# Lists of 112 places with the tokens in steps of seven, in the expert loop of a decoder trunk

## The chip, the cores and the metric

The kernel runs on one core of a Trainium2 chip. The metric is the device time of one execution in microseconds (us); the median of several executions is compared. The engines are TensorE (PE, with its weight loads as PEld), VectorE (DVE), ScalarE (ACT), GpSimd (POOL) and SyncE (SP, which issues DMAs). The core has 16 DMA engines.

## What is computed

Two layers, each a token mixer (three kinds of attention), a norm, a mixture of experts and a second norm, for 512 tokens of width 1024 in float32. The part that matters here is the mixture of experts:

```
scores = sigmoid(x @ router_w)                    # 512 x 64
idx    = top_k(scores + router_bias, 8)           # 8 of 64 experts for each token
gates  = scores[idx] / sum * 2.5
for each expert e, for the tokens routed to it:
    y = (silu(h @ w1[e]) * (h @ w3[e])) @ w2[e]   # 1024 -> 256 -> 1024
    y = y * gate
out = sum over a token's 8 experts + shared expert
```

In all 512 x 8 = 4096 pairs of a token and an expert arise in each layer, 64 for an expert on average. The weights of one expert are three matrices of 1024 x 256 float32, 1.049 MB each.

## The kernel before

The program runs `_setup` once, and then for each of the two layers `_projections`, `_attention`, `_mix_and_route`, `_experts` and `_second_norm`. Each is a block in which every engine has its own instruction stream, ordered against the others by semaphores.

**Lists.** Each expert has a list of `CAP` = 100 places (line 54). `_mix_and_route` writes into `posm` the rank of each token within each expert's tokens (0, 1, 2, ..., or a negative number if it isn't routed there). For an expert, DVE compares this rank with the constants in `number` (line 1400: `hot` is 1 where the rank equals the place's number); `number` comes from `np.arange(CAP)` in `_constants` (line 106), so the token of rank r stands at place r. A matmul of `hot` with the table `parts` (line 1320, and one with `ones` at 1323) then gives for every place the token's row in `x1_rows`, its destination row in `y_rows` and its gate; a place without a token gets an index that is out of bounds. DVE writes the indices (lines 1408 and 1410). If an expert had more than `CAP` tokens, the expert loop would run again for the rest (`passes`, from the largest count, line 1133); here one pass is run per layer.

**The loop.** `_experts` runs 64 steps, with `Turn(x)` for the expert of the step. The parts of one step lie on different engines:

- SP, `load` (lines 1257 to 1266): the three weight matrices of expert x into slot x mod 4, `w1` and `w3` (1261, 1262) when `up_made` says that PE is through with the slot's last `w1` and `w3`, `w2` (1266) when `down_made` says so. SP's stream is in order, so the `w1` of x + 1 stands behind the wait of `w2` of x.
- POOL, `gather` (line 1287): an indirect DMA of the rows in the list, 4 KB each, from `x1_rows` in HBM, three steps ahead; `put` (line 1295): an indirect DMA of the result rows to `y_rows` in HBM, two steps behind. Rows of places without a token are left out by the bounds check.
- ACT: `up_hi` in two halves (line 1481) rounds the weights to the type that PE multiplies fast (float32r), `hidden_hi` (1502), `gates` (1508, silu), `rows_hi` (1495, 1496), `dn_hi` (1488), `scaled` (1516, multiplies by the gate). In a step they stand in the order up_hi(x+1, 0), hidden_hi(x-1), gates(x), rows_hi(x+1), up_hi(x+1, 1), dn_hi(x), scaled(x-1).
- DVE: `hots` (1400), `indices`, `hidden_lo` (1448), `up_lo` (1429), `hide` (1422), `rows_lo` (1441), `dn_lo` (1434): the differences that the rounding leaves, and the product silu(up) * up.
- PE: `pick` (1320, 1323), `up` in two parts (1347 to 1349, 24 matmuls with 512 columns, three for each exact product: hi*hi, hi*lo, lo*hi), `turn_hidden` (1358, two transposes), `turn_rows` (1332, eight transposes), `down` (1372 to 1374, 12 matmuls). The list is on the stationary side of the matmuls and the weights move.

`silu` is a tile of its own of 128 x 2 x 256 (line 1236), `hidden` the same memory. `w_chunk` (line 1650) holds the first chunk of the projection weights: it is loaded in `_setup` and, for the next layer, in `_second_norm` (line 1570), and is read in `_projections`.

Of the kernel before, what the change touches and what calls it, by code (L numbers as in the profile page):

```python
# [33 lines left out]
P = 128  # L34
# [11 lines left out]
NE, TOPK, FF, SFF = 64, 8, 256, 256  # L46
# [4 lines left out]
MLA_SCALE = MQ ** -0.5  # L51
NEG = -1e30
TAKEN = -3e38
CAP = 100
MAX_PASSES = -(-SEQ // CAP)
NOT_ROUTED = 4096.0
ABSENT = 8192.0
# [27 lines left out]
def _buckets(distance):  # L85
    exact = N_BUCKETS // 2
    d = np.maximum(distance, 1).astype(np.float64)
    large = exact + (np.log(d / exact) / math.log(MAX_DISTANCE / exact) * (N_BUCKETS - exact)).astype(np.int64)
    return np.where(distance < exact, distance, np.minimum(large, N_BUCKETS - 1))


def _constants():
    k = np.arange(SPAN + 1)
    dist = SEQ - 1 - k
    causal = dist >= 0
    onehot = ((_buckets(np.maximum(dist, 0))[None, :] == np.arange(N_BUCKETS)[:, None]) & causal)
    count = sum(((dist % d == 0) & (dist <= w)).astype(np.int64) for w, d in DILATIONS)
    logcount = np.where(causal & (count > 0), np.log(np.maximum(count, 1)), NEG)
    addend = np.concatenate([np.repeat(logcount[None], H_DIL, 0),
                             np.repeat(np.where(causal, 0.0, NEG)[None], H_DSA, 0)])  # L100
    p = np.arange(P)
    inv = 10000.0 ** (-np.arange(0, ROPE, 2) / ROPE)
    square = np.concatenate([np.eye(P), p[:, None] < p[None, :], np.ones((P, P))], 1)
    absent = np.zeros((P, PART))
    absent[0, [IDX, DEST]] = ABSENT
    once = np.concatenate([np.eye(P)[::-1], np.repeat(np.arange(CAP)[None], P, 0), np.ones((P, CAP)), absent], 1)
    token = p[:, None] + P * np.arange(NT)[None]
    row = np.concatenate([np.repeat(inv[None], P, 0), token - ABSENT, TOPK * token - 1 - ABSENT], 1)
    mask = np.where(p[:, None] + (SEQ - P) - np.arange(SEQ)[None] >= 0, 0.0, NEG)
    f = np.float32  # L110
    return {
        "c_square": square.astype(f),
        "c_once": once.astype(f),
        "c_row": row.astype(f),
        "c_mask": mask.astype(f),
        "c_onehot": onehot.astype(f),
        "c_addend": (addend / SCALE).astype(f),
    }
# [31 lines left out]
def _setup(nc, d, sb):  # L150
    with ExitStack() as ctx:
# [10 lines left out]
        turns_i = ctx.enter_context(nc.sbuf_tensor("turns_i", [P, NT, ROPE // 2], I32))  # L162
        once = ctx.enter_context(nc.sbuf_tensor("once", [P, P + 2 * CAP + PART], F32))
        bias = ctx.enter_context(nc.sbuf_tensor("bias_set", [P, 10, SEQ], F32))
# [5 lines left out]
        with nc.Block() as block:  # L170
# [48 lines left out]
            def _(dve):  # L219
# [6 lines left out]
                dve.wait_ge(S["consts_in"], 32)  # L226
                dve.tensor_copy(sb["number"][:], once[:, P:P + CAP]).then_inc(S["numbers"], 1)
                dve.tensor_copy(sb["ones"][:], once[:, P + CAP:]).then_inc(S["numbers"], 1)
                dve.wait_ge(S["positions_in"], 32)
# [614 lines left out]
def _mix_and_route(nc, d, sb, l):  # L844
    with ExitStack() as ctx:
# [31 lines left out]
        with nc.Block() as block:  # L877
# [26 lines left out]
            def _(pool):  # L904
# [3 lines left out]
                for k in range(FIRST):  # L908
                    pool.wait_ge(S["index_ready"], k + 1)
                    pool.indirect_dma_start(sb["rows"][0:CAP, k, :], None, d["x1_rows"],  # L910
                                            bass.IndirectOffsetOnAxis(ap=index[0:CAP, k, 0:1], axis=0),
# [308 lines left out]
def _experts(nc, d, sb, l):  # L1220


    with ExitStack() as ctx:
# [4 lines left out]
        T = lambda name, shape, dt=F32: ctx.enter_context(nc.sbuf_tensor(name, shape, dt))  # L1228
# [4 lines left out]
        w2_hi = T("w2_hi", [P, 2, 2, D], F32R)  # L1233
        hot, index, gate = sb["hot"], sb["index"], sb["gate"]
        rows = sb["rows"]
        silu = T("silu", [P, 2, FF])
        hidden = silu
        rowsT_hi, rowsT_lo = T("rowsT_hi", [P, 2, KD, CAP], F32R), T("rowsT_lo", [P, 2, KD, CAP], F32R)
        hiddenT_hi, hiddenT_lo = T("hiddenT_hi", [P, 2, 2, CAP], F32R), T("hiddenT_lo", [P, 2, 2, CAP], F32R)
# [402 lines left out]
def trunk(nc, d, out):  # L1642
    with ExitStack() as ctx:
# [12 lines left out]
        with nc.Fori(0, DEPTH) as l:  # L1656
            with ExitStack() as kept:
                with ExitStack() as routed:
# [31 lines left out]
                    with nc.Fori(0, passes) as _:  # L1690
                        _experts(nc, d, sb, l)
# [24 lines left out]
```

## Time and profile before

| | |
|---|---|
| median of 3 runs | 2382.28 us (2380.42 to 2382.53) |
| the profiled execution's own time | 2378.7 us |
| its span, first to last instruction | 2376.9 us |
| PE busy | 2134.1 us (90%) |
| DVE busy | 1596.6 us (67%) |
| ACT busy | 1353.1 us (57%) |
| POOL busy | 610.4 us (26%) |
| moved by DMA | 595.90 MB, 251 GB/s over the span |
| row queue (q0, issued by POOL) | 46112 packets, 67.23 MB |

Busy shares are averages over stages with different limits. Matmuls are pipelined, so PE's busy time isn't PE at its peak. A wait says which event came last before an instruction started. In the slices of the page one digit stands for a fortieth of the span (59.4 us) and gives tenths of busy time.

### The profile page before, as it was taken

How to read it: one execution, taken by the hardware profiler on the slowest of the kernel's cores; microseconds unless marked ns; L12 is line 12 of the kernel's file. 1: busy time of each engine (PE TensorE's matmuls, PEld its weight loads, DVE VectorE, ACT ScalarE, POOL GpSimd, SP SyncE). 2: the span in 40 equal slices, each digit the busy share in tenths (PEclk: the TensorE clock that was granted, in tenths of full speed). 3: DMA queues.
4: the chain of work that ended last, by engine and by line, in shares of the span. 5: the costliest groups of instructions: out<-in, count | busy, mean ns of one | idle time of the engine just before them, and what ended most of it. 6: DMA issues, size and time to landing. Idle time of an engine off the chain costs nothing. (4 is left out here: it accounts for less than half of the span.)

```text
span 2376.9 us, 31682 instructions
## 1 busy us (share of the span) xinstructions
PE 2134.1 (90%) x10838; PEld 1571.8 (66%) x10838; DVE 1596.6 (67%) x2283; ACT 1353.1 (57%) x1754; POOL 610.4 (26%) x358
## 2 busy tenths in 40 slices
PE   6999999798999999897679999979999999999947
PEld 5788856576676666665367887457766676766633
DVE  2583434797888788786345924248988888888835
ACT  3533721587777777775034356126876777777731
POOL 0012000243333333333311020002433333333323
PEclk9999999899999999999789999999999999999989
DMA  6213043599999999998931230436999999999978
GB/s 197 77 45 151 2 167 125 194 354 346 347 348 337 345 333 336 341 334 297 380 106 54 63 133 3 173 148 249 356 346 345 339 344 338 341 339 339 345 279 333
DMA packets 148475, 595.90 MB, mean 251 GB/s; under 512 B 41957, under 2 KB 68069, under 8 KB 92313
## 3 DMA queue, kind: packets, MB, share of 16 engines
q1 hardware_dynamic: 102264, 527.41, 60.9%
q0 software_dynamic: 46112, 67.23, 9.1%
q8 instruction: 56, 0.92, 0.2%
q14 instruction: 43, 0.34, 0.0%
HBM read 571.23 MB, written 63.46 MB: 267 GB/s over the span
## 5 line engine op out<-in xcount | busy, mean ns | idle before, releaser
L1295 POOL DMA_INDIRECT y_rows<-y,index x128 | 297.0, 2320 | 798.5 <-ACT y L1516 790.0
L1347 PE MATMUL ps_up<-w_hi,rowsT_hi 128*100 128x512 f32 x1024 | 420.6, 411 | 37.3 <-issue 20.4
L1349 PE MATMUL ps_up<-w_hi,rowsT_lo 128*100 128x512 f32 x1024 | 405.8, 396 | 0.0
L1481 ACT CAST w_hi<-w_next 128x2048 fp32r<-128x2048 f32 x128 | 245.7, 1919 | 179.0 <-DMA w_next<-exp_w 169.5
L1481 ACT CAST w_hi<-w 128x2048 fp32r<-128x2048 f32 x128 | 245.3, 1918 | 132.8 <-DMA w<-exp_w 86.6
L1429 DVE TENSOR_TENSOR w_lo<-w,w_hi 128x2048 fp32r<-128x2048 f32 x128 | 292.3, 2285 | 35.9 <-ACT w_hi L1481 35.8
L1429 DVE TENSOR_TENSOR w_next_lo<-w_next,w_hi 128x2048 fp32r<-128x2048 f32 x128 | 292.1, 2282 | 6.3 <-ACT w_hi L1481 6.3
L1372 PE MATMUL ps_y<-w_hi,hiddenT_hi 128*100 128x512 f32 x512 | 211.3, 413 | 70.5 <-issue 66.2
L1347 PEld LDWEIGHTS ps_up<-w_hi,rowsT_hi 128*100 128x100 f32 x1024 | 173.7, 170 | 94.6 <-issue 41.8
L1287 POOL DMA_INDIRECT rows<-x_rows,index x128 | 189.0, 1476 | 122.5 <-issue 61.7
L1349 PEld LDWEIGHTS ps_up<-w_hi,rowsT_lo 128*100 128x100 f32 x1024 | 169.9, 166 | 68.9
L1348 PE MATMUL ps_up<-w_lo,rowsT_hi 128*100 128x512 f32 x512 | 204.5, 399 | 0.0
L1374 PE MATMUL ps_y<-w_hi,hiddenT_lo 128*100 128x512 f32 x512 | 204.1, 399 | 0.0
L1348 PE MATMUL ps_up<-w_next_lo,rowsT_hi 128*100 128x512 f32 x512 | 201.2, 393 | 0.0
L1448 DVE TENSOR_TENSOR hiddenT_lo<-ps_h,hiddenT_hi 128x200 fp32r<-128x200 f32 x128 | 46.9, 366 | 198.2 <-ACT hiddenT_hi L1502 197.7
L1372 PEld LDWEIGHTS ps_y<-w_hi,hiddenT_hi 128*100 128x100 f32 x512 | 86.9, 170 | 106.2 <-issue 75.5
L1332 PEld LDWEIGHTS ps_t<-ident,rows 100*128 100x128 f32 x1024 | 134.6, 202 | 29.9 <-issue 16.2
L1516 ACT ACTIVATE y<-ps_y,gate 100x1024 f32<-100x1024 f32 x128 | 145.2, 1134 | 12.1 <-DMA y_rows<-y,index 8.8
L1332 PE MATMUL ps_t<-ident,rows 100*128 100x100 f32 x1024 | 132.6, 273 | 16.1 <-PEq L139 16.1
L1434 DVE TENSOR_TENSOR w_next_lo<-w_next,w_hi 128x2048 fp32r<-128x2048 f32 x64 | 146.1, 2283 | 0.0
L1441 DVE TENSOR_TENSOR rowsT_lo<-ps_t,rowsT_hi 128x400 fp32r<-128x400 f32 x256 | 133.6, 563 | 0.0
L1488 ACT CAST w_hi<-w_next 128x2048 fp32r<-128x2048 f32 x64 | 123.2, 1925 | 0.0
(244 smaller groups left out, 4299.2 us busy)
## 6 DMA issues: line engine op xcount, KB each, us to landing
w_next<-exp_w SPq DMA_DIRECT2D x204, 1024.0 KB, 18.8
w<-exp_w SPq DMA_DIRECT2D x136, 1024.0 KB, 14.2
w_first<-exp_w SPq DMA_DIRECT2D x34, 1024.0 KB, 19.7
w_last<-exp_w SPq DMA_DIRECT2D x32, 1024.0 KB, 19.6
wbuf<-w_in SPq DMA_DIRECT2D x16, 1024.0 KB, 5.5
got<-y_rows SPq DMA_DIRECT2D x8, 2048.0 KB, 23.4
got<-y_rows SPq DMA_DIRECT2D x16, 1024.0 KB, 26.4
w_out_sb<-w_out SPq DMA_DIRECT2D x2, 4096.0 KB, 19.6
```

What stands on the lines that cost most here:

```text
L1287: pool.indirect_dma_start(rows[0:CAP, x.slot, :], None, d["x1_rows"], bass.IndirectOffsetOnAxis(ap=index[0:CAP, x.step, 0:1], axis=0), bou ...
L1295: pool.indirect_dma_start(d["y_rows"], bass.IndirectOffsetOnAxis(ap=index[0:CAP, x.step, 1:2], axis=0), y[0:CAP, x.slot % 2, :], None, bou ...
L1332: mm = pe.transpose(ps_t[:, k, 0:CAP], rows[0:CAP, x.slot, k::KD], ident_cap)
L1347: pe.matmul(ps_up[b][0:CAP], hi, w_hi, start=(k == 0), stop=False)
L1348: pe.matmul(ps_up[b][0:CAP], hi, w_lo, start=False, stop=False)
L1349: mm = pe.matmul(ps_up[b][0:CAP], lo, w_hi, start=False, stop=(k == KD - 1))
L1372: pe.matmul(y_out, hi, w_hi, start=(j == 0), stop=False)
L1374: mm = pe.matmul(y_out, lo, w_hi, start=False, stop=(j == 1))
L1429: dve.tensor_tensor(w13_lo[x.slot][:, :, k, :], w13[x.slot][:, :, k, :], w13_hi[:, :, k, :].bitcast(F32), ALU.subtract).then_inc(S["up_lo_ ...
L1434: dve.tensor_tensor(w2_lo[x.slot], w2[x.slot], w2_hi[:, x.slot % 2].bitcast(F32), ALU.subtract).then_inc(S["dn_lo"], 1)
L1481: act.copy(w13_hi[:, :, k, :], w13[x.slot][:, :, k, :]).then_inc(S["up_hi_b" if half else "up_hi_a"], 1)
L1516: act.activation(y[0:CAP, x.slot % 2, :], ps_y[0:CAP, :], ACT.Copy, scale=gate[0:CAP, x.step:x.step + 1]).then_inc(S["y_made"], 1)
```

## The change

`CAP` goes from 100 to 112. The constants in `number` are no longer 0, 1, 2, ... but arange(112) as 7 rows of 16, read by columns: 0, 16, 32, 48, 64, 80, 96, 1, 17, ... So the token of rank r stands at place 7 * (r mod 16) + r // 16. All tiles and instructions that have `CAP` in their shape get 112: the gathers and puts, the transposes, `rowsT_hi` and `rowsT_lo`, `hiddenT_hi` and `hiddenT_lo`, `hot`. `MAX_PASSES` becomes 5 where it was 6. `silu` (and with it `hidden`) is no tile of its own but a view of the memory of `w_chunk`.

```diff
-CAP = 100
+CAP = 112
+SPREAD = 7
@@ _constants
-    once = np.concatenate([np.eye(P)[::-1], np.repeat(np.arange(CAP)[None], P, 0), np.ones((P, CAP)), absent], 1)
+    once = np.concatenate([np.eye(P)[::-1], np.repeat(np.arange(CAP).reshape(SPREAD, -1).T.reshape(1, CAP), P, 0), np.ones((P, CAP)), absent], 1)
@@ _experts
-        silu = T("silu", [P, 2, FF])
+        silu = sb["w_chunk"][:].rearrange("p k c -> p (k c)")[:, 0:2 * FF].rearrange("p (s c) -> p s c", s=2)
         hidden = silu
```

## Rows read from the trace of the kernel before

**Rows 1.** The page: span, busy times, DMA share and rate in 40 slices

```profile
span 2376.9 us, 31682 instructions
PE 2134.1 (90%) x10838; PEld 1571.8 (66%) x10838; DVE 1596.6 (67%) x2283; ACT 1353.1 (57%) x1754; POOL 610.4 (26%) x358
...
PE   6999999798999999897679999979999999999947
...
DMA  6213043599999999998931230436999999999978
GB/s 197 77 45 151 2 167 125 194 354 346 347 348 337 345 333 336 341 334 297 380 106 54 63 133 3 173 148 249 356 346 345 339 344 338 341 339 339 345 279 333
```

**Rows 2.** Waits, 600 to 1050 us: us in total, times, longest

```profile
DVE hiddenT_lo L1448 <- ACT hiddenT_hi L1502: 79.0, 41, 4.2
ACT w_hi L1481 <- DMA w_next<-exp_w: 65.3, 20, 5.3
ACT w_hi L1481 <- DMA w<-exp_w: 40.8, 19, 3.3
...
PE ps_y L1372 <- issue: 25.6, 22, 2.7
```

**Rows 3.** SP's timeline, issues of line 1266: start us, us

```profile
502.54 0.34 SPq L1266 DMA_DIRECT2D w_next<-exp_w  x1
...
541.18 0.33 SPq L1266 DMA_DIRECT2D w_next<-exp_w  x1
...
1084.24 0.33 SPq L1266 DMA_DIRECT2D w_last<-exp_w  x1
...
1724.98 0.33 SPq L1266 DMA_DIRECT2D w_next<-exp_w  x1
...
2039.34 0.33 SPq L1266 DMA_DIRECT2D w_last<-exp_w  x1
2050.75 0.33 SPq L1266 DMA_DIRECT2D w_first<-exp_w  x1
2062.65 0.33 SPq L1266 DMA_DIRECT2D w_next<-exp_w  x1
2072.71 0.33 SPq L1266 DMA_DIRECT2D w_next<-exp_w  x1
...
2254.91 0.33 SPq L1266 DMA_DIRECT2D w_last<-exp_w  x1
```

**Rows 4.** Windows: us, busy PE, PEld, DVE, ACT, POOL, PEclk, DMA share, GB/s

```profile
500.00:550.00 50.00, 49.16 (x259) 36.95 (x258) 44.56 (x51) 41.11 (x43) 20.03 (x11) 1.00 1.02 358
...
700.00:750.00 50.00, 46.15 (x238) 34.32 (x237) 42.42 (x46) 36.57 (x36) 17.14 (x9) 1.00 0.98 336
...
1150.00:1170.00 20.00, 20.00 (x48) 8.96 (x47) 7.77 (x3) 0.00 (x0) 9.01 (x4) 0.99 1.00 422
...
1650.00:1700.00 50.00, 50.00 (x265) 37.67 (x264) 46.58 (x51) 41.52 (x42) 21.93 (x11) 1.00 1.01 359
```

**Rows 5.** Short windows, the same columns

```profile
704.00:705.00 1.00, 1.00 (x6) 0.73 (x5) 1.00 (x2) 0.99 (x1) 0.00 (x0) 1.00 0.94 258
...
708.00:709.00 1.00, 1.00 (x7) 0.75 (x6) 0.00 (x0) 0.63 (x1) 0.70 (x2) 1.00 1.02 385
...
1103.00:1104.50 1.50, 1.50 (x10) 1.21 (x9) 1.50 (x2) 1.12 (x4) 0.65 (x1) 1.00 0.44 117
```

**Rows 6.** DMA queues (page, then 1102.9 to 1104.4 us), landings of row DMAs

```profile
q0 software_dynamic: 46112, 67.23, 9.1%
...
q0 software_dynamic: 122, 0.17, 45.0%
...
rows<-x_rows,index POOLq DMA_INDIRECT x134, 13.6
...
y_rows<-y,index POOLq DMA_INDIRECT x128, 11.6
```

**Rows 7.** Instructions with the list's length (480 to 1110 us), two timeline rows

```profile
L1441 DVE TENSOR_TENSOR rowsT_lo<-ps_t,rowsT_hi 128x400 fp32r<-128x400 f32 x118 | 61.6, 562 | 0.0
...
L1400 DVE TENSOR_TENSOR hot<-number,posm 128x400 bf16<-128x400 bf16 x58 | 32.9, 567 | 0.0
...
708.81 1.03 PE L1332 MATMUL ps_t<-ident,rows 100*128 100x100 f32 x8
...
376.87 1.04 PE L940 MATMUL ps_x<-ident,x_sb 128*128 128x128 f32 x8
```

## Prediction

> **What bounds the kernel now.** I read the page first. The span is 2376.9 us, the program's own time in that execution was 2378.7 us, and the median of the runs is 2382.28 us, so 3.6 us lie between the profiled execution and the median; sums are made on the first and 3.6 us are added. The forty slices [rows 1] show two long stretches, slices 9 to 18 and 29 to 38, in which PE and DMA both stand at 9 and the DMA moves 333 to 356 GB/s. These are the bulk of the two passes over the 64 experts, one per layer, some 680 us each, 57% of the span. All that the change can move lies there or at its edges.
>
> Second view: the issues of `w2` loads (line 1266), one per expert, are a clock for the steps [rows 3]. From 502.54 to 541.18 four steps pass in 38.64 us, 9.66 each. From 541.18 to 1084.24 there are 50 steps, 10.86 each; in the second layer 1724.98 to 2254.91 are 49 steps, 10.82 each. So there is a fast pace, 9.66, that the loop can run at, and it is lost after about ten steps.
>
> Third: who waits [rows 2]. In 450 us of the slow pace (some 41 steps) ACT waits 106 us for a weight DMA before line 1481, 2.7 us a step; behind it on ACT stands `hidden_hi`, for which DVE waits 79 us, and PE then stands 25.6 us before the down projection. In the fast stretch PE is busy 49.16 of 50 us [rows 4]. So the fast pace is PE's, and the slow one is the weight stream's.
>
> Fourth: is the stream at its limit? An expert needs 3 x 1.049 MB of weights, and on average 64 rows of 4 KB gathered and 64 put (512 tokens x 8 over 64 experts), 3.670 MB. In 500 to 550 us the DMA moved 358 GB/s at a share of 1.02; in 700 to 750 us 336 GB/s at 0.98; and 1150 to 1170, with plain loads alone, 422 GB/s at 1.00 [rows 4]. Two things are lost in the slow pace. One is seen in single microseconds [rows 5]: at 708 the DMA is at 1.02 and 385 GB/s, at 704, while rows are gathered and put, at 0.94 and 258. The other is how the rows are dealt: with nothing but the row queue moving (1102.9 to 1104.4) the queue holds only 45% of sixteen engines [rows 6], 7.2 of them, at 117 GB/s over 1103 to 1104.5 [rows 5], what 4.4 engines carry at the 26.4 GB/s each of the 422. A list of 100 places has its 64 tokens in places 0 to 63 and 36 void places behind. If the engines take runs of neighbouring places, the ones with the last places get nothing, and the others ten rows in a row. These carry their weights late, and ACT needs a load whole. The steps show it: in the second layer they go 11.41, 11.90, 10.06 from 2039.34 on [rows 3] and the four-step pattern comes back, as a start engine that moves from list to list would make it (four weight slots would too).
>
> The Trainium skill (DMA: Bandwidth & Descriptors, Why a DMA increments its semaphore by 16 and not by 1) says that a transfer is spread over the largest number up to 16 that divides its outer size: 100 places on 10 engines, ten each, and 112 on 16, seven each. The 45% fits the first half of it; nothing in this trace has 112 places. By it the step of seven gives each engine 4 tokens of 64 in either direction, and by its absence (112 dealt as 100 now) the third rival below holds.
>
> **The change, part by part.**
> (a) Spread lists. Number j becomes (j mod 7)*16 + j div 7, so token 16a + b of an expert goes to place 7b + a: each run of seven places holds 4 tokens of 64 and 3 voids. The DMA's work stays the same in bytes. What goes is the unevenness: engines that idle while others have ten rows. I take the pace of the stream then as that of the two stretches in which the share was full, 358 GB/s at 1.02 in the first layer and 359 at 1.01 in the second (1650 to 1700 us) [rows 4]: 3.670 / 0.359 = 10.22 us a step. Bounds: nothing gained, 10.84; and the plain-load rate, 422 GB/s, 8.70 us, which is below PE's floor in (b), so 9.75.
> (b) PE. Its matmuls of 512 columns hold the list in the stationary side, so their length doesn't see 112. The ten transposes per step move 100 columns and will move 112. Eight take 1.03 us at 100 and 1.04 us at 128 where they stand elsewhere [rows 7], ends modelled; the spread of one start to the next is what counts and can't grow by more than 12%: 8 x 0.10 and 2 x 0.09 us, at most 0.12 and at least 0. I take 0.09, as most of the way: floor 9.66 + 0.09 = 9.75 us. It is paid only at PE's pace.
> (c) DVE and ACT. Where the list is the free side, an instruction grows by 12% at most: `rowsT_lo`, 562 ns, by 67 ns twice a step, `hot`, 567 ns, by 68 [rows 7], `hiddenT_lo` with its 200 columns by less than 67: at most 0.27 us on DVE, and ACT's three copies of the same tiles about as much. DVE is busy 44.56 and 46.58 of 50 us in the two fast stretches [rows 4], at most 9.0 of 9.66 us a step; with 0.27 it has 0.5 us left under 9.75. Hidden by PE or by the stream. If that cover goes (a wait chain ACT, DVE, PE without slack), it costs up to 0.5 us a step at PE's pace and nothing at 10.22.
> (d) POOL issues two indirect DMAs a step; 12% more of them lies in an engine that is busy 26% of the span [rows 1]. At most 24 more void places a step are nothing beside 3.67 MB. Zero, hidden by POOL's idle time; without that cover 12% of POOL's 610 us would be 73 us.
> (e) `silu` in `w_chunk`: the chunk is loaded before the projections and again only in the second norm, so no wait is new; the same instruction writes the same 256 columns. Zero; it is what makes room for the 112.
> (f) MAX_PASSES goes from 6 to 5, one small DVE instruction per layer, 0.2 us; one pass stays one (64 steps per layer, no list over 100). The constants grow by 12 KB in the setup, beside other loads. Zero.
>
> **The sum.** 99 slow steps x (10.84 - 10.22) = 61 us. The reserve of filled slots now lasts ten steps at a deficit of 0.6 us (10.25 at 358 GB/s against 9.66), 6 us; at 0.47 (10.22 against 9.75) it lasts 13: 3 more steps x 0.47 x 2 layers = 3 us. The fast steps cost 20 x 0.09 = 2 us. 2378.7 - 61 - 3 + 2 = 2316.7, and with 3.6 us for the median 2320 us.
>
> **The rivals.**
> PE's pace (0.30): an even stream is also a more efficient one, since the engines keep step; single microseconds at 385 to 389 GB/s exist [rows 5] and 376 suffice for 9.75. Then 99 x (10.84 - 9.75) = 108, less 2: 2276 us; with an occasional late load 2268 to 2297. For it: 422 GB/s in plain loads. Against: 336 to 358 in every 50 us with rows in it. The Trainium skill (DMA: Bandwidth & Descriptors, Specifications) gives a limit of about 358 GB/s of HBM for a core; by it 9.75 us is out of reach and the step is 10.25, 2321 us. The 422 GB/s of this trace are above that limit, so I don't let it exclude this rival.
> No effect (0.12): the lists are dealt otherwise than I read it (the pattern comes from the four slots), or what slows the stream is the presence of any row traffic. Then only the costs of (b) to (d) move, hidden: 2376 to 2388 us.
> Slower (0.10): each row gets dearer. The queue of rows takes 9.1% of 16 engines' span [rows 6], 3460 engine-us for 16384 rows, 211 ns a row. Now neighbours in a run of ten are neighbours in token order; afterwards an engine's rows are 16 ranks apart and all sixteen engines switch between row and weight packets in each step. At 128 rows a step on 16 engines, 77 ns more per row eat the whole 0.62 us; from there it is slower. At +150 ns the step is 10.22 + 1.2 = 11.42, 99 x 0.58 = 57 us: 2440 us. For it: rates are lowest while rows move (258 at 704 [rows 5]). Against: at 704 the share was below that of the other microseconds, so part of the loss is idleness.
>
> **How the numbers follow.** The forecast case (stream-bound at 355 to 365 GB/s, steps 10.05 to 10.35) gives 2303 to 2333 and has 0.48; PE's pace 0.30; no effect 0.12; slower 0.10. The likeliest is 2320. The range goes from 2268 (PE's pace) to 2374, where the slower part of the forecast case (a step of 10.5 us, 2350) and the start of "no effect" lie: it leaves out about 0.19. Some 0.2% (4.8 us) is what a measurement of this kernel can tell from no change: below 2377.5 faster 0.83, within 0.08 (most of "no effect"), above 0.09.
>
> **What would show it.** Right: no step pattern of four; steps at 9.75 for the first 13, then near 10.2; ACT's wait at line 1481 down from 2.7 us a step to about 1.2; the row DMAs' landings (13.6 and 11.6 us [rows 6]) down by 3 us or more, since an engine has four rows where it had ten; the row queue alone on more than 10 engines; DMA share at 1.0 in all 50 us windows at about 359 GB/s. PE's pace would show steps of 9.75 to the end and ACT waiting for PE instead of DMA. No effect: landings and pattern as before. Slower: the row queue's share clearly over 9.1%. The forecast is wrong if the full-share rate is not a limit of the DMA engines but itself an effect of their unevenness (then lower time), or if transposes or DVE set a floor above 9.75.

## The result, and the profile after

The change takes the median from 2381.35 us (4 runs of the kernel before beside it) to 2262.55 us (4 runs, 2258.8 to 2263.92): a ratio of 0.950 (0.948 to 0.952). That is 118.8 us faster, 57 us below the forecast and 5 us below the range. It is the rival "PE's pace" that happened, and a little more than it.

The page of the kernel after, against [rows 1]: span, busy times, the slices of PE and DMA, the rates, and the row queue.

```profile
span 2261.7 us, 31680 instructions
...
PE 2111.1 (93%) x10838; PEld 1603.5 (71%) x10838; DVE 1626.6 (72%) x2281; ACT 1378.4 (61%) x1754; POOL 661.8 (29%) x358
...
PE   6999999799999999997779999997999999999957
...
DMA  5312142399999999998931230434999999999978
GB/s 195 93 48 77 83 166 108 111 354 369 381 382 371 372 374 384 380 377 326 376 96 56 66 140 1 175 131 172 366 377 379 381 364 378 375 373 374 370 305 331
...
q0 software_dynamic: 33536, 67.18, 8.9%
```

PE and DMA stand at 9 in the bulk of both layers as they did, but the DMA now moves 354 to 384 GB/s where it moved 333 to 356. The bytes of the row queue are the same and its packets are 12576 fewer.

SP's issues of the `w2` load are again the clock of the steps, against [rows 3] (start us, us; the line has moved by one):

```profile
501.38 0.33 SPq L1267 DMA_DIRECT2D w_next<-exp_w  x1
...
706.06 0.33 SPq L1267 DMA_DIRECT2D w_next<-exp_w  x1
715.81 0.33 SPq L1267 DMA_DIRECT2D w_last<-exp_w  x1
725.57 0.33 SPq L1267 DMA_DIRECT2D w_first<-exp_w  x1
735.30 0.33 SPq L1267 DMA_DIRECT2D w_next<-exp_w  x1
745.04 0.33 SPq L1267 DMA_DIRECT2D w_next<-exp_w  x1
```

The steps are 9.75, 9.76, 9.73 and 9.74 us. The pattern of four is gone and the pace doesn't fall after ten steps: the mean of steps 13 to 60 is 9.75 us in both layers, where before it was 10.87 and 10.83. PE runs the matmul of line 1323 (1324 now) once in each of the 64 steps. From its first start in a layer to its last 621.5 and 624.8 us pass, before 679.9 and 676.3: 109.9 of the 115.2 us by which the spans differ. The other 5.3 lie outside these stretches: 0.8 before the first, 1.5 between the two and 3.1 behind the second.

The waits from 600 to 1050 us, against [rows 2] (us in total, times, longest us):

```profile
POOL y_rows L1296 <- ACT y L1517: 215.8, 46, 4.8
ACT w_chunk L1509 <- PE ps_up L1350: 37.6, 46, 0.9
...
ACT rowsT_hi L1496 <- PE ps_t L1333: 22.7, 46, 0.6
ACT w_hi L1482 <- PE ps_up L1350: 14.1, 46, 0.3
```

ACT's 106 us of waiting for a weight DMA are gone and no wait of the whole list names a DMA. At the same line (now 1482) ACT waits for PE, 0.3 us a time. The windows say the same, against [rows 4] (us, busy PE, PEld, DVE, ACT, POOL, PEclk, DMA share, GB/s):

```profile
500.00:550.00 50.00, 50.00 (x264) 39.23 (x262) 46.73 (x52) 41.96 (x42) 22.07 (x11) 1.00 1.02 370
700.00:750.00 50.00, 50.00 (x262) 39.26 (x261) 46.98 (x52) 41.99 (x42) 22.68 (x11) 1.00 1.01 374
...
1650.00:1700.00 50.00, 50.00 (x262) 39.32 (x261) 46.97 (x55) 41.88 (x42) 22.83 (x11) 1.00 1.02 375
```

PE is busy for the whole of each window. A DMA share of 1.02 stands beside 375 GB/s here and stood beside 358 in [rows 4]. The share, full in both, was read by the prediction as a limit of bytes, and it isn't one.

### The profile page after: what moved, and what is told of

It is laid out like the page before. It is cut to its first block and busy times, and to the rows that moved or that the text cites. A ratio compares the mean times of both kernels' runs of the same rounds, so it can differ in the third digit from the quotient of the medians.

```text
span 2261.7 us, 31680 instructions
## 1 busy us (share of the span) xinstructions
PE 2111.1 (93%) x10838; PEld 1603.5 (71%) x10838; DVE 1626.6 (72%) x2281; ACT 1378.4 (61%) x1754; POOL 661.8 (29%) x358
## 3 DMA queue, kind: packets, MB, share of 16 engines
q0 software_dynamic: 33536, 67.18, 8.9%
## 5 line engine op out<-in xcount | busy, mean ns | idle before, releaser
L1348 PE MATMUL ps_up<-w_hi,rowsT_hi 128*112 128x512 f32 x1024 | 424.0, 414 | 15.0 <-DVE rowsT_lo L1442 14.7
L1350 PE MATMUL ps_up<-w_hi,rowsT_lo 128*112 128x512 f32 x1024 | 406.3, 397 | 0.0
L1348 PEld LDWEIGHTS ps_up<-w_hi,rowsT_hi 128*112 128x112 f32 x1024 | 183.0, 179 | 59.9 <-issue 15.3
L1350 PEld LDWEIGHTS ps_up<-w_hi,rowsT_lo 128*112 128x112 f32 x1024 | 179.9, 176 | 59.9
L1373 PE MATMUL ps_y<-w_hi,hiddenT_hi 128*112 128x512 f32 x512 | 211.2, 412 | 5.4 <-DVE hiddenT_lo L1449 3.9
L1349 PE MATMUL ps_up<-w_lo,rowsT_hi 128*112 128x512 f32 x512 | 203.5, 397 | 0.0
L1349 PE MATMUL ps_up<-w_next_lo,rowsT_hi 128*112 128x512 f32 x512 | 201.7, 394 | 0.0
L1375 PE MATMUL ps_y<-w_hi,hiddenT_lo 128*112 128x512 f32 x512 | 201.3, 393 | 0.0
L1517 ACT ACTIVATE y<-ps_y,gate 112x1024 f32<-112x1024 f32 x128 | 144.4, 1128 | 10.4 <-PE ps_y L1375 10.4
L1442 DVE TENSOR_TENSOR rowsT_lo<-ps_t,rowsT_hi 128x448 fp32r<-128x448 f32 x256 | 146.5, 614 | 0.0
```

The costliest lines, as they stand in the source:

```text
L1348: pe.matmul(ps_up[b][0:CAP], hi, w_hi, start=(k == 0), stop=False)
L1349: pe.matmul(ps_up[b][0:CAP], hi, w_lo, start=False, stop=False)
L1350: mm = pe.matmul(ps_up[b][0:CAP], lo, w_hi, start=False, stop=(k == KD - 1))
L1373: pe.matmul(y_out, hi, w_hi, start=(j == 0), stop=False)
L1375: mm = pe.matmul(y_out, lo, w_hi, start=False, stop=(j == 1))
L1442: o = dve.tensor_tensor(rowsT_lo[:, b, k, :], ps_t[:, k, 0:CAP], rowsT_hi[:, b, k, :].bitcast(F32), ALU.subtract)
```

## The experiments

Three questions: whether the order of the places or their number makes the gain; whether the alias has a part in it; and why the stream runs at more than 359 GB/s. One theory had it that idle engines are the whole cost; the rival, that it is the size of the list. "Places" are the entries of a list, "engines" are DMA engines. A step's time is the mean of steps 13 to 60 of a layer; where one number stands, it is the first layer's, and two are the two layers'.

### The three parts of the change, each alone

Order alone: the list stays at 100 places, numbers go to them in steps of ten.

```diff
-    once = np.concatenate([np.eye(P)[::-1], np.repeat(np.arange(CAP)[None], P, 0), ...
+    once = np.concatenate([np.eye(P)[::-1], np.repeat(np.arange(CAP).reshape(10, -1).T.reshape(1, CAP), P, 0), ...
```

> Lists of 100 places as before, but the tokens in steps of ten: the token of rank r at place 10*(r mod 10) + r div 10. Theory A (a list is dealt to ten DMA engines in runs of ten neighbouring places, and engines with ten rows in a row hold up the weight stream): each of the ten engines now has 6.4 rows where 6.4 engines had ten, so most of the unevenness within a list goes and what stays is that six engines have none; steps of 9.9 to 10.4 us, 2290 to 2335 us. Theory B (the number of engines alone counts, the order inside the list does not): as before, 2381 us, steps of 10.8 us.

Measured: 2297.76 us beside 2381.08, ratio 0.965 (0.963 to 0.967). Steps of 10.15 us in the first layer, 10.12 in the second. So the order alone, with nothing else of the change, gives 83.3 us of the 118.8. It is also the forecast's own case: an even stream that is slower than PE's pace.

112 places without the order (the change, with the old row of places):

```diff
-CAP = 100
+CAP = 112
...
-        silu = T("silu", [P, 2, FF])
+        silu = sb["w_chunk"][:].rearrange("p k c -> p (k c)")[:, 0:2 * FF].rearrange("p (s c) -> p s c", s=2)
```

> Lists of 112 places as after the change, but the token of rank r at place r as before. Theory A: runs of seven places on sixteen engines, always the same ones, so that nine or ten engines carry seven rows of every gather and every put and the others none. An engine with 14 rows a step has 197 KB of weights and 57 KB of rows, 254 KB where the mean is 229: at the pace of before with all engines busy (10.3 to 10.4 us for the mean) 11.4 us a step, slower than before by some 0.6 us a step, 2400 to 2450 us. Theory B: as after the change, 2263 us, steps of 9.75 us.

Measured: 2338.68 us, ratio 0.981 (0.980 to 0.983), steps of 10.48 and 10.55 us. Both theories missed: sixteen engines without an even order give a third of the gain, not a loss and not the whole. The windows from 600 to 1000 us of the kernel before, of the order alone, of the 112 places alone, and of the change, in this order (columns as above):

```profile
600.00:1000.00 400.00, 368.52 (x1882) 274.50 (x1881) 327.63 (x370) 291.38 (x296) 139.75 (x74) 0.99 0.97 341
```

```profile
600.00:1000.00 400.00, 385.55 (x2000) 288.64 (x1999) 349.85 (x392) 311.75 (x314) 149.89 (x79) 1.00 1.02 365
```

```profile
600.00:1000.00 400.00, 379.71 (x1941) 295.60 (x1940) 345.98 (x381) 305.24 (x305) 147.06 (x76) 1.00 0.95 351
```

```profile
600.00:1000.00 400.00, 400.00 (x2095) 314.54 (x2094) 375.71 (x411) 333.76 (x329) 176.62 (x82) 1.00 1.01 378
```

The share tells the two apart: 0.97 and 0.95 without the order, 1.02 and 1.01 with it. The idle engines are real, and the order removes them. But at the same full share the rate is 365 GB/s with 100 places and 378 with 112: something besides idleness is at work. Divided by the share the four rates are 352, 358, 369 and 374 GB/s. So with either order 112 places move some 16 GB/s more for the same busy time, and idle engines cost at least their whole share.

Why my expectation of 11.4 us a step failed can be worked out with a number found later. It had scaled the step by the busiest engine, 254 KB where the mean is 229, from the 10.3 us of the kernel before. From the 9.51 us that the stream with even lists of 112 places takes by itself (below) the same scaling gives 10.55 us, which is what was measured. The picture of engines that are always the same isn't shown by this: it would give a share of about 0.92, and 0.95 was measured.

Which engines get rows was read from packet counts. The 262 row DMAs of a run leave 46112 packets at 100 places [rows 6], 37728 at 104 and 33536 at 112, 105 and 98: 176, 144 and 128 per list. These are 16 x 10 + 16, 16 x 8 + 16 and 16 x 7 + 16: ten places for each of 10 engines, eight for each of 13, seven for each of 16 (15, 14), if each of the 16 engines is padded to that number and has one packet more. So 100 places use ten engines. The Trainium skill (DMA: Bandwidth & Descriptors, Why a DMA increments its semaphore by 16 and not by 1) says that a transfer goes over the largest number up to 16 that divides its outer size; the counts agree with it for 98, 100, 104, 105 and 112 places.

The alias alone: 100 places in the old order, with `silu` in `w_chunk`.

```diff
-        silu = T("silu", [P, 2, FF])
+        silu = sb["w_chunk"][:].rearrange("p k c -> p (k c)")[:, 0:2 * FF].rearrange("p (s c) -> p s c", s=2)
```

> Only the silu tile in the memory of w_chunk, lists as before. Both theories: no difference, 2381 us within 0.2%.

Measured: 2381.07 us, ratio 1.000 (0.999 to 1.001). The alias costs and gives nothing; it makes room.

The change at 104 places, thirteen engines of eight:

```diff
-CAP = 112
-SPREAD = 7
+CAP = 104
+SPREAD = 8
```

> Lists of 104 places, tokens in steps of eight (13 runs of eight). Theory A: thirteen engines with 4.9 rows each, the start moving from list to list; near enough to even for PE's pace, whose floor is lower by eight columns in ten transposes, 9.69 us a step: 2255 to 2265 us. If three idle engines are too many: some slow steps, up to 2290 us. Theory B (the number of engines): 13 lies in the middle between 10 and 16, some 2320 us.

Measured: 2280.51 us, ratio 0.958 (0.957 to 0.960), steps of 9.91 and 9.96 us, 371 GB/s. It lies between ten engines (2297.76) and sixteen (2262.55), in theory A's second case: with 13 engines some steps are still slow.

### The stream alone: kernels with less work for PE

The change runs at PE's pace, so its stream can't be read from its steps. In the following "light" kernels the matmuls with the low halves of the weights, and the subtractions that make these, are left out: `w_lo` is used neither in the up nor in the down projection. PE then needs less time for a step than the stream does. Each of these kernels was executed once. The edit, made to the kernel before, to the order alone and to the change:

```diff
-                        pe.wait_ge(S["up_lo_a"], x.n + 1)
+                        pe.wait_ge(S["up_hi_a"], x.n + 1)
...
-                        pe.matmul(ps_up[b][0:CAP], hi, w_lo, start=False, stop=False)
...
-                            pe.matmul(y_out, hi, w_lo, start=False, stop=False)
...
-                up_lo(Turn(0, 0), 0)
-                up_lo(Turn(0, 0), 1)
...
-                        up_lo(x + 1, 1)
-                    dn_lo(x)
```

> The kernel before without the products with the low halves of the weights (line 1348 and 1373) and without the subtractions that make these halves (lines 1429 and 1434), so that PE needs about 6.9 us a step, DVE under 3 and ACT 8.6, and the weight stream (3.67 MB a step) must be the limit wherever it can't give 427 GB/s. The output lacks these products. Theory C (the even lists let the stream itself run faster than the 358 GB/s of the full stretches): here, with the uneven lists, steps stay at 10.4 to 10.9 us, 337 to 355 GB/s. Theory D (the stream's full rate is the same for every list, and only idle engines were lost): the same here; the two part in the next kernels.

> The same left out, with the lists of 100 places in steps of ten. The stream was the limit in the full kernel too, with 365 GB/s at a share of 1.02. Theories C and D: steps of 10.0 to 10.1 us.

> The same left out from the kernel after the change. Theory C: the stream now shows its own limit below PE's 9.75, as 10 engines to a list gave 365 and 13 gave 370 GB/s; 380 to 400 GB/s, steps of 9.2 to 9.65 us. Theory D: 365 GB/s is the stream's rate whenever no engine idles, and the 378 of the full kernel is within what lists of 112 add by fewer filler packets: steps of 9.7 to 10.0 us, and the full kernel would have been on the edge.

Measured: 2359.04, 2275.02 and 2199.31 us beside 2385.28 of the full kernel before; steps of 10.73, 10.20 and 9.51 us. The same windows of the three, in this order:

```profile
600.00:1000.00 400.00, 308.61 (x1463) 228.64 (x1463) 92.15 (x265) 292.73 (x300) 77.56 (x74) 0.87 0.96 345
```

```profile
600.00:1000.00 400.00, 324.57 (x1539) 240.37 (x1539) 95.31 (x275) 307.07 (x315) 82.83 (x80) 0.87 1.02 365
```

```profile
600.00:1000.00 400.00, 324.92 (x1646) 253.58 (x1646) 110.37 (x295) 333.74 (x338) 82.10 (x84) 0.94 1.01 389
```

PE is busy 309 to 325 of 400 us and DVE about 100, and ACT waits for weight DMAs in all three (61 us of the 400 in the change), so none of them sets the pace. The stream's own rates are 345, 365 and 389 GB/s, of the two theories for the last one (380 to 400 GB/s, or 365 and little more) it is C's. For the first two they are those of the full kernels (341, 365), whose bound was the stream. For the change the light kernel is faster than the full one (9.51 against 9.75 us): there the bound is PE. PEclk is 0.87 to 0.94 here; the pace isn't PE's, so this doesn't enter.

### What raises the rate at a full share

Two readings of 365 against 389: fewer 4-byte packets (void places, padding and ends of lists, 224 a step against 128), or more engines that share a list. Each was changed without the other. A further put with void places only, in every step:

```diff
+                    pool.sem_inc(S["dma_turns"], 1)
+                    pool.indirect_dma_start(d["y_rows"], bass.IndirectOffsetOnAxis(ap=void[0:CAP, 0:1], axis=0),
+                                            y[0:CAP, x.slot % 2, :], None, bounds_check=PLACES - 1, oob_is_err=False
+                                            ).then_inc(S[f"y{x.slot % 2}_out"], 16)
...
```

The waits for a put count 32 where they counted 16, and `void` is a tile of indices that are out of bounds.

> As the light kernel with the even lists of 112 (e7), and behind each put a second one whose 112 places are all void, so that it moves no row: 128 packets of 4 bytes more per step (112 places and 16 completions), no bytes to speak of. Theory S (each 4-byte packet costs its engine some 0.1 us of stream time: 224 of them per step in lists of 100, 160 in lists of 104, 128 in lists of 112; with 0.31 us for a weight packet and 0.16 for a row, 384 x 0.31 + 128 x 0.16 + n x 0.1 gives 10.1, 9.7 and 9.5 us on 16 engines): 128 x 0.1 / 16 = 0.8 us a step more, 10.2 to 10.4 us in the stretch at full share. Theory K (it is the number of engines that share a list which sets the rate, small packets cost the 9 ns that they take): 0.07 us more, 9.4 to 9.5 us.

Measured: 2236.28 us; steps of 9.79 and 9.72 us, against 9.51 in both layers without them. So the 128 further small packets cost 0.28 and 0.21 us a step, and neither expectation (10.2 to 10.4, 9.4 to 9.5 us) came true. That is 4.5 and 3.4 us of one engine's time, 35 and 26 ns a packet, where the packet's own record shows 9 ns (median). With 256 small packets a step, more than the 224 of the light order, it still runs at 377 GB/s.

The light change with lists of 104, 96 and 98 places (13, 16 and 14 engines):

```diff
-CAP = 112
-SPREAD = 7
+CAP = 104
+SPREAD = 8
```

> The light kernel with lists of 104 places in steps of eight. Theory S: 160 small packets a step, 0.2 us over lists of 112: 9.6 to 9.75 us at full share, 376 to 382 GB/s. Theory K: 13 engines, half way between 365 and 389 GB/s, 9.75 us. The two lie close here; it says whether the scale between 100 and 112 is even.

```diff
-CAP = 112
-SPREAD = 7
+CAP = 96
+SPREAD = 6
```

> The light kernel with lists of 96 places in steps of six, 16 runs; it counts for the first layer only (the second may need a second pass). Theory S: 96 small packets a step, 0.2 us under lists of 112, 9.2 to 9.3 us at full share. Theory K: sixteen engines as with 112, no change, 9.4 to 9.5 us.

```diff
-CAP = 112
+CAP = 98
```

> The light kernel with lists of 98 places in steps of seven: 14 runs of seven on 14 engines, and with the fillers of the two others as many small packets a step as with 112 (128). Theory K (the number of engines that share a list sets the full-share rate, since a list of 64 rows is in flight the shorter the more engines carry it): between 13 engines (371 GB/s) and 16 (390), 378 GB/s, steps of 9.75 us. Theory S2 (only the count of small packets, 0.03 engine-us each as the voids kernel showed): as with 112, 390 GB/s, 9.5 us.

Measured: 2257.36 us for 104 places, 2222.74 for 98. The 98 places, at 9.69 us and 383 GB/s, lie between their two expectations, nearer to theory K's. With 96 places the second layer ran a second pass over the experts (2733.17 us in all), so only first passes are compared. The windows of 104, 96 and 98 places, in this order:

```profile
600.00:1000.00 400.00, 319.52 (x1582) 242.10 (x1580) 100.09 (x280) 315.17 (x322) 86.60 (x82) 0.91 1.02 373
```

```profile
600.00:1000.00 400.00, 321.84 (x1633) 237.12 (x1631) 97.76 (x292) 324.14 (x334) 79.24 (x84) 0.93 1.01 386
```

```profile
600.00:1000.00 400.00, 323.81 (x1619) 240.67 (x1618) 100.39 (x293) 322.91 (x330) 83.53 (x82) 0.91 1.02 383
```

Put together, all of light kernels with even lists. For 96 places the second layer's first pass is taken; the small packets follow from the counts per list above:

```
places  engines  small packets a step  step us, layers  GB/s (window)
100     10       224                   10.20, 10.26     365
104     13       160                    9.90, 10.10     373
 98     14       128                    9.69,  9.68     383
 96     16        96                    9.57,  9.55     386
112     16       128                    9.51,  9.51     389
112     16       256                    9.79,  9.72     377
```

98 and 112 places have the same packets and differ in the engines (14, 16): 0.18 us. 96 and 112 have the same engines, and the list with 32 fewer packets isn't faster. 100 and the last row have 224 and 256 packets, and the one with more is 0.41 us faster. So the number of engines decides, and the small packets are the lesser part: from 224 to 128 they are worth 96 x 26 to 35 ns / 16 = 0.16 to 0.21 us of the 0.69 between the first row and the fifth.

Rows left out, in three ways. Light change with only the first 16 places of each list gathered and put; with 16 gathered and all put; with all gathered and 16 put (from the second lap of the ring on; the others stay undone, so the output is another):

```diff
+                    n = CAP if x.known and x.n < LAP else 16
...
-                    pool.indirect_dma_start(rows[0:CAP, x.slot, :], None, d["x1_rows"],
-                                            bass.IndirectOffsetOnAxis(ap=index[0:CAP, x.step, 0:1], axis=0),
+                    pool.indirect_dma_start(rows[0:n, x.slot, :], None, d["x1_rows"],
+                                            bass.IndirectOffsetOnAxis(ap=index[0:n, x.step, 0:1], axis=0),
...
```

Where the puts are cut, `put` has the same `n` in place of `CAP`.

> As the kernel before this one, but from the second lap on gathers and puts take the first 16 places of a list only (y_rows is set once in the setup, some tens of us more there), so that row traffic nearly goes while all waits stay: 3.15 MB of weights and some 0.07 MB of rows a step. Theory C and D in common: the rows cost more than their bytes. If they do, the rate rises towards the 422 GB/s of plain loads and the step is ACT's, 8.6 to 8.8 us, at 365 to 375 GB/s with the DMA share under 1; if they don't, the same.

> The light kernel with lists of 112, gathers cut to the first 16 places from the second lap on, puts whole: 3.4 MB a step. If it is the puts (writes to HBM, two a step per engine in turn with the weights' reads) that hold the stream back, the rate stays at 390 GB/s, 8.75 us a step; if it is the gathers, it rises to 400 GB/s and more, 8.5 us or less; if both alike, 397 GB/s, 8.6 us.

> The same with the puts cut to 16 places and the gathers whole (y_rows is set once in the setup). If it is the puts, 400 GB/s and more, 8.5 us or less; if the gathers, 390 GB/s, 8.75 us. Only the steps of the first layer are compared.

Measured: first-layer steps of 8.11, 8.74 and 8.96 us (the whole times are 2616.93, 2110.59 and 2715.1 us; in the first and the last the second layer ran a second pass, so again only first layers are compared). With both cut the step is near ACT's pace (ACT is busy 385 of 400 us, 396 GB/s), which is 0.5 us less than the expectation had. The last kernel is the light change with no gather at all: a plain load of 64 neighbouring rows of `x1_rows`, the same ones in every step, by the same queue stands in its place, and 16 places are put.

```diff
-                    pool.indirect_dma_start(rows[0:CAP, x.slot, :], None, d["x1_rows"],
-                                            bass.IndirectOffsetOnAxis(ap=index[0:CAP, x.step, 0:1], axis=0),
-                                            bounds_check=SEQ - 1, oob_is_err=False).then_inc(S[f"rows{x.slot}_in"], 16)
...
+                        pool.dma_start(rows[0:64, x.slot, :], d["x1_rows"][64:128, :]).then_inc(S[f"rows{x.slot}_in"], 16)
```

> As e14 (few places put, light kernel), but from the second lap on the gather is replaced by a plain load, issued by POOL on the same queue, of 64 neighbouring rows of x1_rows into the first 64 partitions: the same bytes, four rows on each of sixteen engines, no void places and no scattering. If the scattering or the void places of the gather cost the stream its rate: steps fall from 8.96 to 8.6 us or less, 400 GB/s and more while rows are in flight. If any second reading queue does: 8.9 to 9.0 us, 345 to 350 GB/s while rows are in flight. Only the steps of the first layer are compared.

Measured: 2227.28 us, steps of 9.32, slower than either expectation. The windows of few gathered, few put, and plain rows, in this order:

```profile
600.00:1000.00 400.00, 328.00 (x1692) 256.58 (x1690) 113.67 (x305) 343.00 (x348) 82.08 (x88) 0.93 0.98 389
```

```profile
600.00:1000.00 400.00, 334.26 (x1751) 261.76 (x1750) 117.81 (x313) 353.43 (x359) 83.85 (x90) 0.97 1.02 390
```

```profile
600.00:1000.00 400.00, 328.47 (x1670) 256.01 (x1669) 112.73 (x299) 339.36 (x345) 60.62 (x86) 0.94 1.02 374
```

From the records of single packets between 600 and 1000 us: in which share of the time no packet of a 4 KB row is in flight on any engine, the rate in that time, and the rate in the rest.

```
kernel                     no row in flight   GB/s then   GB/s otherwise
before                          0.24             378          330
order alone                     0.28             394          354
104 places                      0.39             406          348
112 places, plain order         0.35             405          323
the change                      0.42             406          358
light order                     0.28             394          353
light change                    0.51             408          369
light, 16 gathered              0.69             387          395
light, 16 put                   0.67             413          345
light, plain rows, 16 put       0.64             409          312
```

While rows are in flight, all the traffic of the core together is slower, 354 to 358 GB/s against 394 to 406 in the order alone and the change. The weighted rates give the windows back: 0.28 x 394 + 0.72 x 354 = 365, 0.42 x 406 + 0.58 x 358 = 378. So a list that passes through all engines at once is done sooner and leaves the stream alone for 0.42 of the time instead of 0.28. But that is only a part of the gain. With the rates of both states held at their means, the shares alone give 0.14 x 44 = 6 of the 13 GB/s, and from the light order to the light change 0.23 x 40 = 9 of the 24. The rest is that both states are faster. In the light kernels the fewer small packets have some 6 to 8 GB/s of it (an estimate from their price above); what the remainder is isn't shown.

The two kernels with one direction cut say which rows these are, though not by their whole rates: 389 and 390 GB/s are as much as the light change moves (389), and by the expectations the first of them would stand for the puts and the second for the gathers. The time with rows in flight parts them. With the puts whole and few gathers the rate with rows in flight is no lower than without (395 and 387; ACT is busy 343 of 400 us there and the share is 0.98, so this stream is in part held up by its user). With the gathers whole and few puts it falls from 413 to 345. The steps agree: each of the two moves about 0.22 MB a step less than the light change, by an estimate 0.57 us at 389 GB/s; few puts save 0.55 us, few gathers 0.77. So the gathers cost the stream more than their bytes, and for the puts no such cost is seen. It takes neither scatter nor voids, because plain loads of neighbouring rows (the same in every step) do worse (312). Nor is it only the engine that carries the row: in the kernel with few puts a weight packet of 8 KB that starts with no row in flight takes 313 ns (median) and one that starts beside six to nine rows 411, though at a share of 1.02 each engine has hardly more than one packet in flight, so that most of these packets are on other engines. In the light change, where gathers and puts are mixed, the medians don't show it (313 and 309), only the means (319 and 356). Why reading rows of 4 KB from `x1_rows` slows the weight loads of other engines stays open; another pitch of `x1_rows` wasn't tried, nor were 128 places.

### Is there a better length?

105 places in steps of seven are fifteen engines, with shorter transposes than 112. The edit, to the full kernel of the change:

```diff
-CAP = 112
+CAP = 105
```

> The whole computation, lists of 105 places in steps of seven, 15 runs on 15 engines. PE's floor falls with seven columns less in ten transposes, to some 9.70 us a step. If the stream with 15 engines holds 378 GB/s beside a full PE: 128 x 0.05 = 6 us under the kernel after the change, 2257 us. If it does not (theory K, between the 370 GB/s of 13 engines and what 16 have to spare): slow steps come back in part, 2262 to 2275 us.

Measured: 2261.34 us (2257.14 to 2263.54), ratio to the kernel before 0.950 (0.948 to 0.951), steps of 9.75 us: the same as the change. No version here beats it.

## Why the prediction was wrong, step by step

**What bounds the kernel: right.** The stream bound the slow steps and PE the fast ones. The order alone, which touches nothing of PE's work, took 83.3 us away, and the light kernel before, with PE's work cut, stayed at 10.73 us.

**(a) Spread lists: mechanism right, rate wrong. This is the step that failed.** It took 359 GB/s, that of the stretches with a full share, as what an even stream moves, 10.22 us a step. It named itself what would make that wrong, a full-share rate that is an effect of uneven lists, and that was found only in its smaller part. Two terms were mis-sized. Idle engines gone, at ten engines a list, gives 365 GB/s (10.15 us), 6 above the value taken; the fast stretches of the kernel before had uneven lists as well. And the list on 16 engines instead of 10 gives the stream another 24 (389 GB/s, 9.51 us), a term that the sum didn't have: it counted bytes and idle time, and not on how many engines the rows lie. The sum's own division, 3.670 MB by the rate, would give 10.05 and 9.43 us for the two, a little under the measured steps. With 10.15 in place of 10.22 the sum gives 2313; the order alone measured 2298, and the 15 between the two haven't been taken apart in full; as below, the edges have a part in them (80.0 us of span were gained, 75.4 of them in the steps). The second term then crosses PE's floor.

**The limit of 358 GB/s.** The prediction set the Trainium skill's limit of about 358 GB/s of HBM for a core (DMA: Bandwidth & Descriptors, Specifications) beside the 422 GB/s of [rows 4] and didn't let it exclude the rival, which was right; but the forecast's 359 had come out next to it. The row gives the figure as half of a stack's 716 GB/s. The windows of 400 us at 378 and 389 GB/s show that this core, alone at work, isn't held to it. By that figure the prediction had 2321 us; its own terms give 2324.

**(b) PE's floor: the number right, by luck.** 9.66 + 0.09 = 9.75, measured 9.75. But the 0.09 isn't the transposes. In the first steps, at PE's pace, it takes 0.81 us from the start of the eight transposes to the start of the next matmul with 100 columns and with 112, and [rows 7] had shown 1.03 and 1.04 us for 100 and 128, which spoke for zero. What grew from the kernel before to the one after, in the mean of six such steps, are the twelve matmuls of the down projection with 0.04 us, the 24 of the up projection with 0.03 and `pick` with 0.02; in all of these the list is the stationary side, of which the prediction had said that its length isn't seen. Their weight loads are longer (PEld at line 1347, 100 columns, against 1348, 112 columns, below), and whether that is the cause isn't shown. 104 and 105 places took 9.72 and 9.74 us in such steps. DVE's instruction with the list's length has grown as it said, from 562 to 614 ns on the mean of the whole page:

```profile
L1347 PEld LDWEIGHTS ps_up<-w_hi,rowsT_hi 128*100 128x100 f32 x1024 | 173.7, 170 | 94.6 <-issue 41.8
...
L1348 PEld LDWEIGHTS ps_up<-w_hi,rowsT_hi 128*112 128x112 f32 x1024 | 183.0, 179 | 59.9 <-issue 15.3
...
702.21 1.04 PE L1333 MATMUL ps_t<-ident,rows 112*128 112x112 f32 x8
...
L1442 DVE TENSOR_TENSOR rowsT_lo<-ps_t,rowsT_hi 128x448 fp32r<-128x448 f32 x256 | 146.5, 614 | 0.0
```

**(c) DVE and ACT: right.** DVE is busy 47.0 of 50 us, hidden under PE's 50.0.

**(d) POOL and void places: zero in the time of this kernel, not in the stream.** POOL's busy time went from 610 to 662 us, all of it beside other work. 128 void packets more cost the light stream 0.21 to 0.28 us a step; but the number of small packets has fallen, from 224 to 128 a step, since the padding went with the even division.

**(e) `silu`: right**, 0.0 us by the alias alone. **(f)** wasn't measured by itself; the two DVE instructions fewer are on the page (x2281 against x2283).

**The rivals.** PE's pace gave 2276 and its range began at 2268. It was short by 13.5 us. The steps gained 109.9 us where its sum has 106, since the slow pace was taken from one part of each layer (10.84; the means are 10.87 and 10.83) and 99 slow steps were counted where there are a few more. Outside the steps 5.3 us were gained, of which it counted none. The rest, about 4, are the 3.6 us that it added for the median and the difference between executions. "Each row dearer" didn't happen: the row queue's time is 8.9% of the span, 3221 engine-us, where it was 3460. Its fear, packets of one engine 16 ranks apart, is not seen. "No effect" was excluded by the order alone. (The prediction calls it the third rival where it speaks of 112 places dealt as 100; it is the second.)

**What was to show it.** No pattern of four: seen. Row DMAs landing 3 us sooner: the puts' median from 600 to 1000 us went from 11.7 to 8.7; for the gathers of the kernel after the trace gives no landing there. ACT's wait of 2.7 us was one per wait, 106 us in 39; a step it was 2.6. Steps falling to 10.2 after 13: not seen, and in the order alone seen as 10.15.

## What to carry to other kernels

Look at how many DMA engines a list with one place per row is dealt to, from the packets of its queue, and choose a length that divides by 16, with the occupied places spread over all of the runs (15 engines were as good here only because PE was the bound). A DMA share of 1.0 is no limit of bytes: compare the rate with that of another stretch at full share, and ask what else is in flight. And a rate taken from a good stretch of the old kernel is a lower bound, if what the change removes is in that stretch too.

## What the runs showed of the hardware

- Idle engines cost the rate at least their whole share: with 100 places 341 GB/s at 0.97 and 365 at 1.02, with 112 places 351 at 0.95 and 378 at 1.01. At a full share the light stream moved 365 GB/s with lists on 10 engines, 373 on 13, 383 on 14 and 389 on 16.
- A gather of 4 KB rows lowers the rate of everything in flight, from 413 to 345 GB/s with few puts; puts of such rows don't. Weight packets that started beside six to nine such rows took 411 ns instead of 313.
- Void places and padding of an indirect DMA are packets of 4 bytes and cost 26 to 35 ns of one engine each, where their own records show 9. A list of 100 places leaves 176 packets, one of 112 leaves 128.
- One core's DMA held 389 GB/s for 400 us with mixed traffic.
- Eight transposes of a list took PE 0.81 us with 100 columns and with 112; the matmuls with the list on the stationary side grew instead, by 0.09 us a step.
